# One head's mean of squares: from one fp32 product to two F32R products, placed two slices later

## The chip, the cores and the metric

One NeuronCore of one Trainium2 chip runs the whole program. The metric is the device time of one execution in microseconds (us); lower is better. Engines are named as the profile names them: PE (TensorE's matrix products), PEld (its weight loads), DVE (VectorE), ACT (ScalarE), POOL (GpSimd), SP (SyncE, which only issues DMAs here).

## The reference

The program is a whole network on one sequence of 512 tokens and 1024 features: a first block (convolutions, an RG-LRU, an MLP) and a second one (a gated linear recurrence, an MLP, latent attention, an MLP). The change lies in the recurrence of the second block, `hgrn2_mixer`. Cut to what matters:

```python
q = silu(xn @ w_q);  forget = lb + (1 - lb) * sigmoid(xn @ w_f);  k = 1 - forget;  v = xn @ w_i
# per head (8 heads of 128): o = decayed q.k scores within a chunk @ v, plus q @ carried state
o = o.reshape(1, 512, 8, 128)
o = o * rsqrt(mean(o * o, axis=-1) + 1e-6) * g_norm      # the mean of a head's squared outputs
o = (o * silu(xn @ w_g)).reshape(1, 512, 1024)
return o @ w_o
```

The kernel computes it to fp32's accuracy: a large product is taken as three F32R products of high and low parts (high times high, high times low, low times high).

## The kernel before

Everything is kept with features on the 128 partitions and the 512 tokens along the row. The program of each engine is written out by hand, in order, with semaphores; nothing is scheduled by a compiler. Each engine runs its own list strictly in order, so an instruction that waits holds up all that stands behind it.

Weights come in chunks of 128x2048 through two slots (`raw`, slot 0 and slot 1). ACT makes the high part `w_hi` of a chunk (`split_hi`, L698) when PE is done with the chunk that was in the slot, and POOL makes the low part `w_lo` (`split_lo`, L648) when ACT is done. PE waits for POOL's part (`chunk_in`). In the recurrence a head needs two chunks: slot 0 holds the weights of q and of the forget gate, slot 1 those of the out gate and of v.

The recurrence works on two heads at once. While PE does head h, it fits the projections of head h+1 in as slices; a slice is one of the 8 contraction steps of two output tiles, 6 products of 128x512. `head_pe(h)`:

1. `gates_pe(h+1)`, 8 slices from slot 0, with `mean_out(h-1)` in between: a product with a matrix of ones adds the squares over the partitions (one fp32 product, before the third slice)
2. `turn_values`, `turn_keys` (transposes), `diagonal`
3. seven times `level(h, l)` and behind each a slice of `rest_pe(h+1)` from slot 1; the first of these slices (L2061 behind level 0) is the first reader of slot 1's new chunk
4. `outputs(h)` into bank 6

`level(h, l)` from l=2 on waits until DVE has copied the results of two levels before (`h_g_free`, L1726 and L1729). Head 7 is the last: its slices belong to the output projection (`out_slices`), and only six of them stand ahead of `turn_values`.

DVE, for head h, in `head_dve(h)`: the two gates of head h+1 (L1715, L1716), the copies of the levels (L1726, L1729), then the decays, keys and values of h+1, then `decayed_dve(h+1)`: 14 products (L1794, L1795) and L1799; then the norm of head h: L1834 (needs the inverse root), L1838 (times the out gate), L1840 (low part `OL`, needs ACT's `OH`), L1842 (a scaling of `X` that belongs to the residual). L1838, L1840 and L1842 read two operands from SBUF, as L1794, L1795 and L1799 do; L1777, L1778, L1715, L1716 and L1834 read one of theirs from PSUM.

ACT, for head h: square of head h's outputs (L1032), then for the next head: logarithm and exponential of the mean (`root_out`, L1037, L1039), `split_hi` of slot 1 (L698), `OH` (L1044), `split_hi` of slot 0 (L698), copies of values and keys (L1055, L1057), then gates and decays.

POOL does nothing but the two `split_lo` of each head. The two heads of the loop body and the peeled heads 0 and 7 run the same functions.

Of the kernel before, what the change touches and what calls it, by code (L numbers as in the profile page):

```python
# [7 lines left out]
P = 128  # L8
T = 512
TB = T // P  # L10
D = 1024
KD = D // P
# [17 lines left out]
F32 = mybir.dt.float32  # L30
# [80 lines left out]
def build_program(nc, a, out):  # L111
    ctx = ExitStack()
    with ctx:
# [10 lines left out]
        def sem(name):  # L124
# [69 lines left out]
            ("HE", [P, 7, T], F32), ("HP", [P, T], F32), ("HQD", [P, 2, T], F32), ("HKD", [P, 2, T], F32),  # L194
            ("HEB", [P, 2, T], F32), ("reset", [P, T], F32),
            ("HKT", [P, 3, P], F32), ("HS", [P, 3, P], F32), ("masks", [P, 9 * 256], U8),
            ("FR", [P, T], F32),
        ]
        at_h, made = base + 16 * TILE, []
        for name, shape, dt in tiles_of:  # L200
            made.append(place(name, shape, dt, at_h)[0])
            size = int(np.prod(shape[1:])) * (1 if dt == U8 else 4)
            at_h += size + (-size) % 32
        HR, HZ, HQ, HK, HF, HGATE, HVF, HV, HE, HP, HQD, HKD, HEB, reset, HKT, HS, masks, FR = made

        AH, _ = place("AH", [P, HEADS_M, T], F32R, a_xh)
        AL, _ = place("AL", [P, HEADS_M, T], F32R, S)
# [49 lines left out]
        def s_(name):  # L257

            if name not in S_:
                S_[name] = sem(name)  # L260
            return S_[name]
# [13 lines left out]
            "t_made": ("z_scaled", 8), "t_hi": ("vg_lo", 12), "t_lo": ("v_done", 12), "part_done": ("lru_m", 12),  # L275
            "part_kept": ("lru_done", 15), "u_y": ("mu_add", 7), "u_f": ("xc_done", 8), "u_fh": ("uh_done", 8),
            "u_fl": ("yb_evac", 8), "root_2": ("ch_done", 2), "d_scaled": ("v_part", 36),
        }

        def ff(name, value=0):  # L280
# [3 lines left out]
        def ff_sem(name):  # L284

            return ff(name)[0]
# [406 lines left out]
        def _(act):  # L693
# [335 lines left out]
            def square_out(h):  # L1029

                act.wait_ge(s_("h_o"), h + 1)
                act.activation(tmp[:, 0], ps[:, 6], ACT.Square).then_inc(s_("h_sq"), 1)  # L1032

            def root_out(h):

# [30 lines left out]
                square_out(h)  # L1066

            act.sem_inc(s_("h_ms"), 1)
            gates_act(0, first=True)
            decays_act(0, 0, first=True)  # L1070
            head_act(0, 0, first=True)
# [168 lines left out]
        def _(dve):  # L1240
# [533 lines left out]
            def rest_dve(h, n):  # L1774

                dve.wait_ge(halves, half_at(2 * h + c + 1, 1))
                dve.tensor_tensor(HVF[:], ps[:, 3], HR[:], ALU.mult).then_inc(s_("h_vf"), 1)  # L1777
                dve.tensor_tensor(HGATE[:, n], ps[:, 2], HR[:], ALU.mult).then_inc(s_("h_g0"), 1)  # L1778
# [6 lines left out]
            def decayed_dve(h, n, levels=range(len(LEVELS)), last=True):  # L1785
# [12 lines left out]
                dve.wait_ge(s_("h_eb"), h + 1)  # L1798
                dve.tensor_tensor(HQD[:, n], HQ[:], HEB[:, n], ALU.mult).then_inc(s_("h_qd"), 1)  # L1799

            def keep_dve(s):

                dve.wait_ge(lo_done, FIRST["hwo"] + s + 3)
                for half, w in enumerate((w_hi, w_lo)):
                    dve.tensor_copy(XH[:, 6 + s, half * 256:half * 256 + 256], w[:, s, 7 * 256:8 * 256])\
                        .then_inc(s_("h_kept"), 1)

            def head_dve(h, n, more=True, first=False):
                if more and not first:
                    gates_dve(h + 1)  # L1810
                levels_dve(h, range(2 if first else 0, 4))
                if more:
                    floor_dve(h + 1)
                else:
                    keep_dve(0)
                levels_dve(h, (4,))
                states_dve(h, n)
                levels_dve(h, (5,))
                if more:
                    scan_dve(h + 1)  # L1820
                else:
                    keep_dve(1)
                levels_dve(h, (6,))
                if more:
                    to_end_dve(h + 1, 1 - n)
                    decays_dve(h + 1, range(3))
                levels_dve(h, (7,))
                if more:
                    decays_dve(h + 1, range(3, len(LEVELS)))
                    keys_to_end_dve(h + 1, 1 - n)  # L1830
                    rest_dve(h + 1, 1 - n)
                    decayed_dve(h + 1, 1 - n)
                dve.wait_ge(s_("h_inv"), h + 1)
                dve.scalar_tensor_tensor(tmp[:, 1], ps[:, 6], col("hgrn_g_norm_2"), rst[:, 1], ALU.mult, ALU.mult)\  # L1834
                    .then_inc(s_("h_t1"), 1)
                dve.wait_ge(s_("h_t1"), h + 2)
                dve.wait_ge(s_("hg_done"), h + 1)
                dve.tensor_tensor(tmp[:, 1], tmp[:, 1], HGATE[:, n], ALU.mult).then_inc(s_("h_t2"), 1)  # L1838
                dve.wait_ge(s_("oh_done"), h + 1)
                dve.tensor_tensor(OL[:, bass.ds(h, 1)], tmp[:, 1:2], OH[:, bass.ds(h, 1)].bitcast(F32), ALU.subtract)\  # L1840
                    .then_inc(s_("ho_done"), 1)
                dve.scalar_tensor_tensor(X[:, bass.ds(h, 1)], X[:, bass.ds(h, 1)], dcol("g_final", h),  # L1842
                                         FR[:].rearrange("p (a t) -> p a t", a=1), ALU.mult, ALU.mult)
# [176 lines left out]
        def _(pe):  # L2020
# [298 lines left out]
            def gates_pe(h, ks=range(KD)):  # L2319

                chunk_in(2 * h + c)
                pair(0, 0, XH, XL, lambda k: at("n_hg", "lo", k + 1), ks)
# [88 lines left out]

            def mean_out(h):

                pe.wait_ge(s_("h_sq"), h + 1)
                pe.matmul(ps[:, 7], ones[:], tmp[:, 0], start=True, stop=True).then_inc(s_("h_mean"), 1)

            def head_pe(h, n, more=True, first=False):
                pe.wait_ge(s_("h_q0"), h + 1)
                pe.wait_ge(s_("h_f0"), h + 1)
                if more:  # L2420
                    gates_pe(h + 1, range(2))
                else:
                    out_slices(0, 0, range(2))
                if not first:
                    mean_out(h - 1)
                if more:
                    gates_pe(h + 1, range(2, KD))
                else:
                    out_slices(0, 0, range(2, 6))
                turn_values(h)  # L2430
                turn_keys(h, n)
                diagonal(h)
                pe.wait_ge(s_("h_g0"), h + 1)
                for l in range(len(LEVELS)):
                    level(h, l)
                    if more:
                        rest_pe(h + 1, range(l, l + 1))
                    elif l < 3:
                        out_slices(1, 2, range(l, l + 1))
                    elif l == 3:  # L2440
                        out_slices(0, 0, range(6, 7))
                    else:
                        out_slices(1, 2, range(l - 1, l))
                    if l == 2:
                        states(h, n)
                if more:
                    rest_pe(h + 1, range(7, KD))
                outputs(h, n)
                if not more:
                    out_slices(1, 2, range(6, 7))  # L2450
                    out_slices(2, 4, range(1))
                    mean_out(h)
                    out_slices(2, 4, range(1, 7))
                    for n_ in range(2):
                        out_closed(n_, 2 * n_)
                    out_slices(2, 4, range(7, KD))
# [336 lines left out]
```

## Time and profile before

| | |
|---|---|
| median of 3 runs | 2184.43 us (2183.82 to 2184.82) |
| profiled execution, its own time | 2183.96 us |
| its span, first to last instruction | 2182.2 us |
| around the span | 1.8 us |
| granted TensorE clock, mean | 1.000 (2.4 GHz) |
| PE busy | 2165.0 us, 99% |
| DVE / ACT / POOL busy | 1461.6 / 998.0 / 939.0 us |
| the recurrence, roughly | 874 to 1160 us of the span |

Read it so: PE is busy nearly all the time, so a change shows in the time as far as it takes work or waiting off PE or puts it there. What the other engines do costs nothing until PE has to wait for it.

### The profile page before, as it was taken

What the parts mean: (1) busy time and instruction counts of PE and PEld (TensorE: products, weight loads), DVE (VectorE), ACT (ScalarE), POOL (GpSimd) and SP (SyncE); (2) the same over time, 40 slices, a digit from 0 to 9 for tenths busy, and PEclk for the clock granted to TensorE, in tenths of its full rate; (3) what the DMA queues carried; (4) which work ended last, traced back from release to release, by engine and by line L of the source; (5) the groups of instructions that cost most, each with busy time, mean ns of one, the idle gap of its engine ahead of it and who ended that gap; (6) DMA issues with size and microseconds to landing.
All of it is one profiled execution on the core that took longest, in us unless ns stands there. A gap on an engine that the chain in (4) does not pass through costs nothing.

```text
span 2182.2 us, 30303 instructions
## 1 busy us (share of the span) xinstructions
PE 2165.0 (99%) x11542; PEld 1840.1 (84%) x11542; DVE 1461.6 (67%) x1980; ACT 998.0 (46%) x1364; POOL 939.0 (43%) x263
## 2 busy tenths in 40 slices
PE   8999999999999999999999999999999999999998
PEld 6888888888898897888888898898788888898897
DVE  6999998777556468878877556467666514556463
ACT  5353554525343344666645343344566524343343
POOL 3444455544553554323134553554411244553552
PEclk9999999999999999999999999999999999999999
DMA  5233332422233333222113223332322233323331
GB/s 200 97 106 106 106 116 82 147 90 96 97 102 102 107 97 107 59 78 58 58 58 97 97 97 97 98 110 85 102 53 58 70 85 97 97 97 97 98 112 72
DMA packets 230851, 206.67 MB, mean 95 GB/s; under 512 B 13904, under 2 KB 220368, under 8 KB 230480
## 3 DMA queue, kind: packets, MB, share of 16 engines
q1 hardware_dynamic: 227328, 199.36, 29.5%
q10 hardware_dynamic: 3408, 5.70, 0.7%
q8 instruction: 81, 1.33, 0.3%
q14 instruction: 34, 0.28, 0.0%
HBM read 194.02 MB, written 4.19 MB: 91 GB/s over the span
## 4 chain that ended last, share of the span: by engine, by line
PE 92%; issue 4%; POOL 2%; ACT 1%; DVE 1%; DMA 0%; POOLq 0%; SPq 0%; ACTq 0%; DVEq 0%
PE ps L2028 15%; PE ps L2029 15%; PE ps L2030 15%; PE ps L2261 6%; PE ps L2259 6%; PE ps L2260 6%; PE ps L2061 5%; PE ps L2063 5%; PE ps L2062 5%; PE ps L2388 2%; POOL w_lo L648 2%; PE ps L2595 2%; PE ps L2556 2%; PE ps L2584 1%; PE ps L2691 1%
## 5 line engine op out<-in xcount | busy, mean ns | idle before, releaser
L648 POOL TENSOR_TENSOR w_lo<-raw,w_hi 128x2048 fp32r<-128x2048 f32 x145 | 692.1, 4773 | 944.4 <-ACT w_hi L698 934.5
L698 ACT ACTIVATE w_hi<-raw 128x2048 fp32r<-128x2048 f32 x144 | 275.8, 1915 | 530.4 <-PE ps L2030 354.9
L2028 PE MATMUL ps<-FH,w_hi 128*128 128x512 f32 x528 | 208.3, 395 | 0.0
L2029 PE MATMUL ps<-FL,w_hi 128*128 128x512 f32 x528 | 208.3, 395 | 0.0
L2030 PE MATMUL ps<-FH,w_lo 128*128 128x512 f32 x528 | 208.2, 394 | 0.0
L2028 PE MATMUL ps<-XH,w_hi 128*128 128x512 f32 x512 | 203.2, 397 | 0.0
L2029 PE MATMUL ps<-XL,w_hi 128*128 128x512 f32 x512 | 202.1, 395 | 0.0
L2030 PE MATMUL ps<-XH,w_lo 128*128 128x512 f32 x512 | 202.0, 395 | 0.0
L661 POOL TENSOR_TENSOR w_lo<-raw,w_hi 128x1024 fp32r<-128x1024 f32 x39 | 107.8, 2765 | 198.0 <-ACT w_hi L892 198.0
L1605 DVE TENSOR_TENSOR ps<-ps,rst 128x1024 f32<-128x1024 f32 (+1 forms) x52 | 55.4, 1066 | 171.4 <-PE ps L2030 122.4
L1341 DVE SCALAR_TENSOR_TENSOR ps<-UP,vec,ps 128x512 f32<-128x512 f32 x224 | 148.6, 744 | 0.0
L2061 PE MATMUL ps<-XH,w_hi 128*128 128x512 f32 x352 | 146.2, 415 | 0.9 <-POOL w_lo L648 0.9
L2063 PE MATMUL ps<-XH,w_lo 128*128 128x512 f32 x352 | 138.8, 394 | 0.0
L2062 PE MATMUL ps<-XL,w_hi 128*128 128x512 f32 x352 | 138.7, 394 | 0.0
L891 ACT ACTIVATE w_hi<-raw 128x1024 fp32r<-128x1024 f32 x39 | 41.4, 1061 | 203.8 <-PE ps L2030 166.7
L1582 DVE TENSOR_TENSOR tmp<-ps,SN 128x512 f32<-128x512 f32 x39 | 27.0, 691 | 157.3 <-PE ps L2261 157.3
L671 POOL TENSOR_TENSOR FL<-tmp,FH 128x1024 fp32r<-128x1024 f32 x36 | 90.0, 2501 | 75.8 <-ACT FH L924 75.8
L2028 PEld LDWEIGHTS ps<-FH,w_hi 128*128 128x128 f32 x528 | 99.5, 188 | 23.3
L2030 PEld LDWEIGHTS ps<-FH,w_lo 128*128 128x128 f32 x528 | 99.5, 188 | 23.3
L2029 PEld LDWEIGHTS ps<-FL,w_hi 128*128 128x128 f32 x528 | 99.5, 188 | 23.2
L2029 PEld LDWEIGHTS ps<-XL,w_hi 128*128 128x128 f32 x512 | 96.4, 188 | 23.2 <-issue 0.7
L2028 PEld LDWEIGHTS ps<-XH,w_hi 128*128 128x128 f32 x512 | 96.4, 188 | 23.1 <-issue 0.7
(435 smaller groups left out, 5896.2 us busy)
## 6 DMA issues: line engine op xcount, KB each, us to landing
raw<-in_w SPq DMA_DIRECT2D x64, 512.0 KB, 4.1
raw<-in_mlp_w_up SPq DMA_DIRECT2D x64, 512.0 KB, 4.7
raw<-in_mlp_w_down SPq DMA_DIRECT2D x64, 512.0 KB, 4.3
raw<-in_w_in SPq DMA_DIRECT2D x56, 512.0 KB, 4.6
raw<-in_mla_w_o SPq DMA_DIRECT2D x16, 512.0 KB, 5.1
raw<-in_w_b_out SPq DMA_DIRECT2D x16, 384.0 KB, 3.9
raw<-in_w_a_out SPq DMA_DIRECT2D x8, 512.0 KB, 4.3
raw<-in_w_o SPq DMA_DIRECT2D x8, 512.0 KB, 4.0
```

Source lines behind the costliest of these rows:

```text
L648: pool.tensor_tensor(w_lo[:, s], raw[:, s], w_hi[:, s].bitcast(F32), ALU.subtract)\
L698: act.activation(w_hi[:, s], raw[:, s], ACT.Copy).then_inc(hi_done, 1)
L1341: dve.scalar_tensor_tensor(dst, src, w, acc, ALU.mult, ALU.add).then_inc(cs, 1)
L2028: pe.matmul(dst, his[k], xh[k], start=start and k == 0, stop=False)
L2029: pe.matmul(dst, his[k], xl[k], start=False, stop=False)
L2030: mm = pe.matmul(dst, los[k], xh[k], start=False, stop=stop and k == n - 1)
L2061: pe.matmul(dst, h[n][k], xh[:, k], start=k == 0, stop=False)
L2062: pe.matmul(dst, h[n][k], xl[:, k], start=False, stop=False)
L2063: mm = pe.matmul(dst, l[n][k], xh[:, k], start=False, stop=k == KD - 1)
L2259: pe.matmul(dst, his[k], ah[k], start=start and k == 0, stop=False, skip_group_check=True)
L2260: pe.matmul(dst, his[k], al[k], start=False, stop=False, skip_group_check=True)
L2261: mm = pe.matmul(dst, los[k], ah[k], start=False, stop=k == 3, skip_group_check=True)
```

## The change

The mean of a head's squares is no longer one fp32 product but two F32R ones, of the squares' high part and low part, both with ones in F32R. ACT makes the high part (a copy, right behind the square), DVE the low part (a subtraction, put ahead of `decayed_dve(h+1)`). PE's wait is now for DVE's low part, and `mean_out(h-1)` stands four slices into the gates of the next head and not two. At the end, for head 7, its place stays.

```diff
+            ("FR", [P, T], F32), ("ONES", [P, P], F32R),
+        SQ, _ = place("SQ", [P, 2, T], F32R, a_tmp + 2 * TILE)
...
                 act.activation(tmp[:, 0], ps[:, 6], ACT.Square).then_inc(s_("h_sq"), 1)
+                act.wait_ge(s_("h_sq"), h + 1)
+                act.activation(SQ[:, 0], tmp[:, 0], ACT.Copy).then_inc(ff_sem("h_sqh"), 1)
...
+            act.activation(ONES[:], ones[:], ACT.Copy).then_inc(ff_sem("ones_hi"), 1)
             gates_act(0, first=True)
...
+            def low_square_dve(h):
+
+                dve.wait_ge(*ff("h_sqh", h + 1))
+                dve.tensor_tensor(SQ[:, 1], tmp[:, 0], SQ[:, 0].bitcast(F32), ALU.subtract).then_inc(ff_sem("h_sql"), 1)
...
                     rest_dve(h + 1, 1 - n)
+                low_square_dve(h)
+                if more:
                     decayed_dve(h + 1, 1 - n)
...
             def mean_out(h):
-                pe.wait_ge(s_("h_sq"), h + 1)
-                pe.matmul(ps[:, 7], ones[:], tmp[:, 0], start=True, stop=True).then_inc(s_("h_mean"), 1)
+                pe.wait_ge(*ff("ones_hi", 1))
+                pe.wait_ge(*ff("h_sql", h + 1))
+                pe.matmul(ps[:, 7], ONES[:], SQ[:, 0], start=True, stop=False)
+                pe.matmul(ps[:, 7], ONES[:], SQ[:, 1], start=False, stop=True).then_inc(s_("h_mean"), 1)
...
                 if more:
-                    gates_pe(h + 1, range(2))
+                    gates_pe(h + 1, range(4))
                 else:
-                    out_slices(0, 0, range(2))
+                    out_slices(0, 0, range(4))
                 if not first:
                     mean_out(h - 1)
                 if more:
-                    gates_pe(h + 1, range(2, KD))
+                    gates_pe(h + 1, range(4, KD))
                 else:
-                    out_slices(0, 0, range(2, 6))
+                    out_slices(0, 0, range(4, 6))
```

On PE the place is the gates in the loop body. `XH`, `XL` are the high and low parts of the input, `w_hi`, `w_lo` those of the weights. Before, two slices (12 products) stand between `outputs` and the mean:

```order
L2407 MATMUL ps<-HP,HV 128x128
L2409 MATMUL ps<-HQD,HS 128x128
...
L2061 MATMUL ps<-XH,w_hi 128x512
L2062 MATMUL ps<-XL,w_hi 128x512
L2063 MATMUL ps<-XH,w_lo 128x512
L2414 REGISTER_ALU
L2415 MATMUL ps<-tmp,ones 128x512
L2061 MATMUL ps<-XH,w_hi 128x512
L2062 MATMUL ps<-XL,w_hi 128x512
```

Now four slices (24 products) stand ahead of it:

```order
L2073 MATMUL ps<-XH,w_hi 128x512
L2074 MATMUL ps<-XL,w_hi 128x512
L2075 MATMUL ps<-XH,w_lo 128x512
L2428 MATMUL ps<-SQ,ONES 128x512
L2429 MATMUL ps<-SQ,ONES 128x512
L2073 MATMUL ps<-XH,w_hi 128x512
L2074 MATMUL ps<-XL,w_hi 128x512
```

So 12 products moved from behind the mean to ahead of it, and all that waits for the mean moved with it.

On ACT the place is the end of a head and the beginning of the next, with the line numbers of the changed kernel (before: L1032, L1037, L1039, L698, L1044):

```order
L1034 ACTIVATE tmp<-ps 128x512
L1036 ACTIVATE SQ<-tmp 128x512
L1041 ACTIVATE rst<-ps,vec 128x512
L1043 ACTIVATE rst<-rst 128x512
L698 ISA
L699 ISA
L700 ACTIVATE w_hi<-raw 128x2048
L1048 ISA
L1048 ACTIVATE OH<-tmp 128x512
```

The copy is new; `split_hi` of slot 1 still stands behind the exponential of the mean's root.

On DVE the place is ahead of the 14 products of `decayed_dve` (before: L1778, then L1794):

```order
L1782 TENSOR_TENSOR HVF<-ps,HR 128x512
L1783 TENSOR_TENSOR HGATE<-ps,HR 128x512
L1809 TENSOR_TENSOR SQ<-tmp,SQ 128x512
L1798 ISA
L1799 TENSOR_TENSOR HE<-HE,HK 128x4x64
L1800 TENSOR_TENSOR HE<-HE,HQ 128x4x64
```

L1809 is new and moves everything behind it back.

## Rows read from the trace of the kernel before

**Rows 1.** The page, busy time of each engine.

```profile
PE 2165.0 (99%) x11542; PEld 1840.1 (84%) x11542; DVE 1461.6 (67%) x1980; ACT 998.0 (46%) x1364; POOL 939.0 (43%) x263
```

**Rows 2.** Waits of PE, 880 to 1170: waiter, releaser, total us, times, longest.

```profile
PE ps L2061 <- POOL w_lo L648: 0.9, 1, 0.9
```

**Rows 3.** Timeline of PE, one head: start, us, engine, line, op.

```profile
1086.20 0.39 PE L2063 MATMUL ps<-XH,w_lo 128*128 128x512 f32 x1
1086.42 1.02 PE L2415 MATMUL ps<-tmp,ones 128*128 128x512 f32 x2
...
1087.51 0.39 PE L2062 MATMUL ps<-XL,w_hi 128*128 128x512 f32 x1
...
1095.42 0.39 PE L2063 MATMUL ps<-XH,w_lo 128*128 128x512 f32 x1
...
1098.12 0.47 PE L2061 MATMUL ps<-XH,w_hi 128*128 128x512 f32 x1
...
1101.87 1.00 PE L2388 MATMUL ps<-HE 128*128 128x64 f32 x8
```

**Rows 4.** Timeline of ACT, the same head.

```profile
1084.38 0.58 ACT L1032 ACTIVATE tmp<-ps 128x512 f32<-128x512 f32 x1
1087.48 0.69 ACT L1037 ACTIVATE rst<-ps,vec 128x512 f32<-128x512 f32 x1 [2.53 <-PE ps L2415]
...
1088.74 1.91 ACT L698 ACTIVATE w_hi<-raw 128x2048 fp32r<-128x2048 f32 x1
1096.06 0.63 ACT L1044 ACTIVATE OH<-tmp 128x512 f32 x1 [5.41 <-DVE tmp L1838]
1096.60 1.89 ACT L698 ACTIVATE w_hi<-raw 128x2048 fp32r<-128x2048 f32 x1
```

**Rows 5.** Timeline of POOL, the same head.

```profile
1090.73 4.65 POOL L648 TENSOR_TENSOR w_lo<-raw,w_hi 128x2048 fp32r<-128x2048 f32 x1 [20.83 <-ACT w_hi L698]
1098.57 4.60 POOL L648 TENSOR_TENSOR w_lo<-raw,w_hi 128x2048 fp32r<-128x2048 f32 x1 [3.19 <-ACT w_hi L698]
```

**Rows 6.** Timeline of DVE, the same head.

```profile
1084.93 0.68 DVE L1778 TENSOR_TENSOR HGATE<-ps,HR 128x512 f32<-128x512 f32 x1
1085.52 0.41 DVE L1794 TENSOR_TENSOR HE<-HE,HK 128x256 f32<-128x256 f32 x1
...
1091.60 4.33 DVE L1838 TENSOR_TENSOR tmp<-tmp,HGATE 128x512 f32<-128x512 f32 x1
1096.85 0.69 DVE L1840 TENSOR_TENSOR OL<-tmp,OH 128x512 f32 x1 [0.92 <-ACT OH L1044]
1097.46 0.74 DVE L1842 SCALAR_TENSOR_TENSOR X<-X,vec,FR 128x512 f32 x1
...
1100.17 1.05 DVE L1729 COPY_PREDICATED HP<-masks,ps 128x256 f32<-128x256 uint8 x2
```

**Rows 7.** Timeline of POOL and of DVE from 889: one POOL instruction that took longer.

```profile
889.24 8.51 POOL L648 TENSOR_TENSOR w_lo<-raw,w_hi 128x2048 fp32r<-128x2048 f32 x1 [7.28 <-ACT w_hi L698]
889.29 0.42 DVE L1771 TENSOR_TENSOR HE<-HF 128x256 f32<-128x256 f32 x1
...
893.25 0.68 DVE L1777 TENSOR_TENSOR HVF<-ps,HR 128x512 f32<-128x512 f32 x1
```

**Rows 8.** Timeline of POOL and of DVE at 421, in an earlier stage.

```profile
421.43 4.86 POOL L648 TENSOR_TENSOR w_lo<-raw,w_hi 128x2048 fp32r<-128x2048 f32 x1 [3.78 <-ACT w_hi L698]
421.13 5.70 DVE L1480 TENSOR_TENSOR XL<-CO,XH 128x512 fp32r<-128x512 f32 x2
```

**Rows 9.** Timeline of POOL and PE, last head: slot 1's chunk and its first slice.

```profile
1123.99 4.62 POOL L648 TENSOR_TENSOR w_lo<-raw,w_hi 128x2048 fp32r<-128x2048 f32 x1 [20.83 <-ACT w_hi L698]
1128.66 0.51 PE L2028 MATMUL ps<-OH,w_hi 128*128 128x512 f32 x1
```

**Rows 10.** Timeline of POOL and of DVE, end of head 0.

```profile
924.11 5.34 POOL L648 TENSOR_TENSOR w_lo<-raw,w_hi 128x2048 fp32r<-128x2048 f32 x1 [15.65 <-ACT w_hi L698]
925.67 4.33 DVE L1838 TENSOR_TENSOR tmp<-tmp,HGATE 128x512 f32<-128x512 f32 x1
```

More of the change, by code:

```diff
@@ L196, in build_program @@
             ("HKT", [P, 3, P], F32), ("HS", [P, 3, P], F32), ("masks", [P, 9 * 256], U8),
-            ("FR", [P, T], F32),
+            ("FR", [P, T], F32), ("ONES", [P, P], F32R),
         ]
+        SQ, _ = place("SQ", [P, 2, T], F32R, a_tmp + 2 * TILE)
         at_h, made = base + 16 * TILE, []
@@ L203, in build_program @@
             at_h += size + (-size) % 32
-        HR, HZ, HQ, HK, HF, HGATE, HVF, HV, HE, HP, HQD, HKD, HEB, reset, HKT, HS, masks, FR = made
+        HR, HZ, HQ, HK, HF, HGATE, HVF, HV, HE, HP, HQD, HKD, HEB, reset, HKT, HS, masks, FR, ONES = made
         AH, _ = place("AH", [P, HEADS_M, T], F32R, a_xh)
@@ L277, in build_program @@
             "u_fl": ("yb_evac", 8), "root_2": ("ch_done", 2), "d_scaled": ("v_part", 36),
+            "h_sqh": ("mu_mm", 1), "h_sql": ("mu_done", 1), "ones_hi": ("var_mm", 1),
         }
```

## The prediction

> **What bounds the kernel now.** I read the page first: PE is busy 2165.0 of 2182.2 us, 99% of the span [rows 1]. So a gain can only be PE's own work, and a loss is any wait that reaches PE. The waits of the recurrence come next: PE waits there for anything nameable only once, 0.9 us for POOL's low part [rows 2]. Then I read the timelines of the four engines over one head, because the change is small on PE and larger in what it moves on the others. The head from 1086 on stands for the rest: the same POOL instruction comes 33.26 us later in the next head [rows 5, 9]. Two things are to be seen.
>
> First, PE's list. The product of the mean starts at 1086.42, and the second product behind it at 1087.51; the next 34 products take 7.91 us, 0.233 each [rows 3].
>
> Second, DVE and POOL get in each other's way. L1838 takes 4.33 us where L1840, of the same form, takes 0.69 [rows 6]. It began at 1091.60, POOL's subtraction ran from 1090.73 to 1095.38 [rows 5], and L1838 ended at 1095.93, 0.55 behind it. So a DVE instruction with two operands in SBUF stands still while POOL's subtraction runs. L1834, with an operand in PSUM, does not. Today this costs nothing: PE has other work.
>
> **The change part by part.** *The product itself.* The fp32 mean costs 1087.51 - 1086.42 - 0.23 = 0.86 us. Two F32R products cost 0.46. That is 0.40 less, 8 times in the program: 3.2 us saved on PE, the whole of the intended gain. The copy of the ones (128x128) at the start of the recurrence lies in ACT's time before the first gates are scaled; without that cover it would cost less than L1044's 0.63 [rows 4], once.
>
> *The mean's date.* 12 products move ahead of it, 2.78 us. It starts at 1089.20 and its second product ends at 1089.20 + 0.23 + 0.39 = 1089.82 (before: 1087.44). L1037 starts 0.04 behind, at 1089.86, where it was 1087.48 [rows 4]: 2.38 later. `split_hi` of slot 1 is queued behind it on ACT and moves with it, and POOL's first subtraction with that: from 1090.73 to 1093.11 and, at 4.6 us, to 1097.7.
>
> *The squares' parts.* ACT ends the square at 1084.96 [rows 4]; the copy, priced as L1044 at 0.63, ends at 1085.62. DVE starts 0.16 behind (as L1840 behind L1044: 1096.69 to 1096.85), at 1085.78, and gives way after 0.60. The products of `decayed_dve` begin at 1086.38 and not at 1085.52 [rows 6]: all of DVE's list moves by 0.86. PE has its low part at 1086.5, long before 1089.20, so the new wait itself costs nothing; the cover is the two added slices. At the end, for head 7, there are only two slices, and the low part would be there some 0.4 us before PE.
>
> *Who is late next.* L1838 now starts at 1091.60 + 0.86 = 1092.46, before POOL (1093.11), and is done at 1093.15: 2.8 us earlier than before. `OH` follows on ACT, 1093.3 to 1093.9. L1840 could go at 1094.07 but now it is the one that POOL holds, to 1097.7, and it ends 0.55 later, at 1098.25, where it ended at 1097.54. Behind it on DVE stand L1842, the gates of the next head, and the level copies.
>
> Meanwhile ACT is free for `split_hi` of slot 0 as soon as PE has left the slot. The last product of the gates starts at 1095.42 - 0.40 and ends at 1095.41; ACT works to 1097.4, POOL's second subtraction is due at 1097.45. Before, ACT came to it only at 1096.60, and POOL began at 1098.57 [rows 5], 3.19 us after its first one ended and clear of L1840 and L1842. Now it is due 0.25 us before the first one ends. POOL's two instructions, 9.2 us together, touch, and DVE has two two-operand instructions to get in at the joint.
>
> If POOL goes on with the second at the joint or takes the gap of some hundredths of a us between L1840 and L1842, then L1842 stands from 1098.2 to the end of the second subtraction, 1102.75, and ends 0.55 later, at 1103.3; before it ended at 1098.20 [rows 6]. All of DVE behind it is 5.1 us late: the first L1729 ends at 1100.17 + 0.43 + 5.1 = 1105.7. PE stands at level 2, which it began at 1101.87 [rows 3], until 1105.8. That is 3.9 to 4.1 us more than before for such a head, PE's 0.40 already in it; I take 4.0.
>
> Does POOL get in? The rows are of two kinds. At 889.24 a POOL instruction was due while DVE ran two-operand instructions back to back; it took 8.51 us, that is, it began work at 893.2, when DVE came to L1777 with its operand in PSUM [rows 7]: the 11 DVE instructions from 889.29 on all went ahead of it. At 421.43 it took 4.86, so it began 0.26 us after it was due, between two L1480 that stood back to back; the second ended behind it, both took 5.70 [rows 8]. So either may win. In rows 7 nearly all of DVE's instructions have 256 elements, in rows 8 they have 512, as L1840 and L1842 do. I take POOL as the winner.
>
> The Trainium skill has a rule for this ("SBUF — State Buffer", section Who interferes with whom): whoever issues first gets the shared port for the whole instruction, and the other blocks until it finishes. Rows 8 go with it, rows 7 against it. By the rule L1840 (waiting since 1094.07) would come ahead of POOL's second, and the second (due 1097.45) ahead of L1842: the same case and the same sum.
>
> *How often.* Both `split_hi` stand in heads 1 to 6, so six pairs. The first is different: there POOL would be due at 924.11 + 2.38 = 926.49 and L1838 at 925.67 + 0.86 = 926.53 [rows 10]. If POOL is first there, L1838 is held as before, `OH` is late, slot 0's split and the values' copy behind it on ACT come 1.7 us later than before, and PE loses about that; if not, it is a pair like the others. I take 1.7. Five pairs at 4.0 are 20.0.
>
> *The last head.* PE's first slice from slot 1 began at 1128.66, 0.05 behind POOL's end at 1128.61 [rows 9]: here POOL was already just in time, because only six slices stand ahead. POOL comes 2.38 later, so does the slice; a wait of 0.2 behind it falls away. 2.1 us lost, the saving of that head's mean included. In the other heads the slice stands at 1098.12 - 0.40 = 1097.72 against POOL's 1097.7 + 0.05: up to 0.1 each, hidden where PE stands at level 2 anyway. The mean of head 7 saves 0.40.
>
> Sum: 20.0 + 1.7 + 2.1 - 0.4 = +23.4 us on the profiled execution's 2183.96 us (span 2182.2 and 1.8 around it), which lies 0.5 us below the median of the runs, 2184.43. I predict 2207.
>
> **The rivals.** *No collision that counts (not slower).* DVE gets in at the joint with L1840 and L1842 both, as in rows 7. L1840 ends at 1098.25, L1842 starts at 1098.17 and not at 1097.46, the first L1729 ends at 1101.3, PE wants level 2 at 1101.5: a tie, up to 0.1 us. Then a head costs -0.40 + 0.1 + 0.1 = -0.2, five of them -1.0; the first pair +1.7 or nearly nothing, the last head 2.1, the last mean -0.4: +0.7 to +2.4, 2185 to 2187. It decides at one point: who holds the port between 1097.7 and 1098.2 of a head. Rows 7 speak for it, rows 8 against.
>
> *The saving alone.* If all the waits that I add (the last head too) were hidden, 3.2 us would be gained: 2181.2. Against it: rows 9, where nothing hides POOL.
>
> *POOL ahead of L1838 in all heads.* It needs 0.65 us less between them than I find. Then L1838 is held to 1098.25, every head is like the first pair, 1.7 each: +12, 2196.
>
> **How the numbers follow.** A measurement here tells a change from none from about 0.2%, 4.4 us. Collision: 0.52, its own range 2200 to 2213. DVE wins at both: 0.36, 2183 to 2188. Saving alone: 0.05. POOL ahead of L1838, or a collision in some heads only: 0.07, 2190 to 2199. The range has to hold both main cases: 2183 to 2213. Slower takes the first, the last and a rest of the second: 0.6. Same 0.37; faster 0.03, since 3.2 us is less than 4.4.
>
> **What would show it.** PE's waits in the recurrence: some 4 us at level 2 of heads 2 to 6, for DVE's copy; in the last head 2.4 us for POOL at the first slice from slot 1. L1842's counterpart at 5 us or L1840's at 8; L1838's back at 0.69. POOL's two instructions touching, 9.2 us. The two new products 0.23 apart. If instead both DVE instructions stand between POOL's two, the collision step is wrong and the rest holds. The whole is wrong if L1840's counterpart is never held, that is, if ACT or POOL comes at other dates than the chain from the mean gives.

## The result and the profile after

The changed kernel takes **2226.59 us** (median of 4 runs, 2225.38 to 2227.31), the kernel before, in the same session, 2184.12 us (4 runs, 2183.72 to 2184.82). The ratio is 1.0194 with a 95% interval of 1.0178 to 1.0210: 1.9% slower. The forecast was 2207 in a range of 2183 to 2213. The direction was right, the size was not: the loss is 42 us and not 23. The profiled execution took 2225.38 us with a span of 2223.6, 41.4 us more than the span before.

The page of the changed kernel, busy time of each engine (it answers to [rows 1]):

```profile
PE 2179.0 (98%) x11542; PEld 1853.6 (83%) x11542; DVE 1492.0 (67%) x1988; ACT 1004.2 (45%) x1373; POOL 940.2 (42%) x263
```

PE has as many instructions as before, and they should be 3.2 us shorter. Yet PE is busy 14 us longer. So there are two losses: PE stands (that is, it waits with nothing to do), and PE works more slowly.

Waits of PE in the recurrence, 870 to 1210, in the changed kernel: waiter, releaser, total us, times, longest (answers to [rows 2]):

```profile
PE ps L2400 <- DVE HP L1734: 24.5, 6, 4.1
PE ps L2040 <- POOL w_lo L650: 2.5, 1, 2.5
PE ps L2073 <- POOL w_lo L650: 1.3, 2, 1.0
```

Six stands at level 2, one for each pair of POOL instructions, and one in the last head. The next four fences show what leads to such a stand. First POOL, ACT and DVE of the changed kernel, the head from 1082 on (they answer to [rows 5], [rows 4] and [rows 6]; L1850, L1852 and L1854 are L1838, L1840 and L1842 of before):

```profile
1085.29 9.57 POOL L650 TENSOR_TENSOR w_lo<-raw,w_hi 128x2048 fp32r<-128x2048 f32 x2 [30.45 <-ACT w_hi L700]
```

```profile
1082.05 0.69 ACT L1041 ACTIVATE rst<-ps,vec 128x512 f32<-128x512 f32 x1 [4.24 <-PE ps L2429]
...
1083.31 1.90 ACT L700 ACTIVATE w_hi<-raw 128x2048 fp32r<-128x2048 f32 x1
1085.35 0.63 ACT L1048 ACTIVATE OH<-tmp 128x512 f32 x1
1087.65 1.91 ACT L700 ACTIVATE w_hi<-raw 128x2048 fp32r<-128x2048 f32 x1 [1.67 <-PE ps L2075]
```

```profile
1083.75 0.74 DVE L1846 SCALAR_TENSOR_TENSOR tmp<-ps,vec,rst 128x512 f32<-128x512 f32 x1
1084.53 0.69 DVE L1850 TENSOR_TENSOR tmp<-tmp,HGATE 128x512 f32<-128x512 f32 x1
1086.14 4.29 DVE L1852 TENSOR_TENSOR OL<-tmp,OH 128x512 f32 x1 [0.92 <-ACT OH L1048]
1090.35 5.06 DVE L1854 SCALAR_TENSOR_TENSOR X<-X,vec,FR 128x512 f32 x1
1095.33 0.68 DVE L1720 TENSOR_TENSOR HZ<-ps,HR 128x512 f32<-128x512 f32 x1
```

POOL's instruction begins 3.24 us behind the mean's root, as before. Its two instructions are one block of 9.57 us now. L1850 runs free in 0.69. L1852 comes 0.85 us behind POOL's start and is held for the first of the two, L1854 for the second. The gates of the next head (L1720, operand in PSUM) start only at 1095.33.

The timeline of PE in the changed kernel, the stand at level 2 and what follows (answers to the last row of [rows 3]):

```profile
1093.24 0.39 PE L2074 MATMUL ps<-XL,w_hi 128*128 128x512 f32 x1
1093.47 0.39 PE L2075 MATMUL ps<-XH,w_lo 128*128 128x512 f32 x1
1097.94 1.96 PE L2400 MATMUL ps<-HE 128*128 128x64 f32 x8 [4.08 <-DVE HP L1734]
...
1100.24 0.63 PE L2074 MATMUL ps<-XL,w_hi 128*128 128x512 f32 x1
1100.66 0.63 PE L2075 MATMUL ps<-XH,w_lo 128*128 128x512 f32 x1
1101.09 0.63 PE L2073 MATMUL ps<-XH,w_hi 128*128 128x512 f32 x1
```

Behind the stand the same products start 0.43 us apart (1100.24, 1100.66, 1101.09), ahead of it 0.23. Busy time by stretch in the changed kernel: after the stretch and its sum the columns are PE, PEld, DVE, ACT and POOL, then the granted TensorE clock, the share of DMA and GB/s:

```profile
930.00:937.50 7.50, 4.71 (x28) 3.72 (x26) 7.50 (x4) 2.39 (x4) 6.00 (x2) 1.00 0.52 143
937.50:944.40 6.90, 5.32 (x19) 4.74 (x20) 2.52 (x6) 6.27 (x8) 0.00 (x0) 0.51 0.55 151
...
978.50:985.30 6.80, 6.50 (x25) 5.93 (x25) 1.37 (x4) 5.69 (x7) 0.00 (x0) 0.50 0.40 108
...
1019.50:1022.90 3.40, 3.40 (x13) 2.92 (x13) 0.81 (x3) 3.33 (x5) 0.00 (x0) 0.50 0.56 146
...
1057.00:1063.80 6.80, 5.87 (x22) 5.30 (x22) 1.86 (x5) 6.14 (x8) 0.00 (x0) 0.50 0.48 132
...
1098.00:1104.80 6.80, 6.80 (x26) 6.22 (x27) 1.14 (x3) 5.33 (x7) 0.00 (x0) 0.50 0.22 74
...
1138.90:1142.30 3.40, 3.40 (x12) 2.86 (x11) 0.76 (x2) 3.35 (x5) 0.00 (x0) 0.50 0.28 97
...
1169.60:1173.00 3.40, 3.40 (x14) 2.93 (x13) 1.77 (x4) 0.00 (x0) 0.00 (x0) 0.51 0.80 247
```

The granted clock is 1.00 in the stretches between them and half of it, that is 1.2 GHz and not 2.4, in seven stretches, each at the end of a stand or behind it. The numbers behind the comma are PE's busy time in them: 5.32 + 6.50 + 3.40 + 5.87 + 6.80 + 3.40 + 3.40 = 34.7 us of work at half rate. How much of it is loss? The products of 512 columns start 0.43 us apart and not 0.23, so a little less than half is lost, 0.20 of 0.43. At 0.46 that is 16.0 us; experiment 4 measures the six falls in the heads directly and finds the same share.

So the account of the profiled execution is: six stands at level 2, +24.5; the last head's wait, +2.5; the other waits for POOL, 1.3 where 0.9 was, +0.4; half rate, +16.0; eight means at 0.40 less, -3.2; and 0.35 for each of the six stands beyond the wait that the profile shows, +2.1. The last term is the rest of a head's length in experiment 4, where the clock did not fall. Nearly half of it is a matter of counting: the wait is counted from the end of the product ahead of it, but the start of L2400 lies 4.47 us behind the start of that product (1093.47 to 1097.94) where 0.23 is usual, which makes 4.24 and not 4.08. The sum is +42.3. The spans differ by 41.4, but this execution reached the recurrence 0.7 us earlier than the one before (POOL's first start behind 870 us is at 876.63, before at 877.34), so from there to the end it lost 42.1.

### The profile page after: what moved, and what is told of

It reads as the page before. It is cut to its first block, busy times and chain, and to the rows that moved or that the text cites. A ratio compares the mean times of both kernels' runs of the same rounds, so it can differ in the third digit from the quotient of the medians.

```text
span 2223.6 us, 30325 instructions
## 1 busy us (share of the span) xinstructions
PE 2179.0 (98%) x11542; PEld 1853.6 (83%) x11542; DVE 1492.0 (67%) x1988; ACT 1004.2 (45%) x1373; POOL 940.2 (42%) x263
## 4 chain that ended last, share of the span: by engine, by line
PE 79%; issue 15%; POOL 3%; DVE 1%; ACT 1%; DMA 0%; POOLq 0%; ACTq 0%; SPq 0%; DVEq 0%
PE ps L2040 14%; PE ps L2042 14%; PE ps L2041 14%; PE ps L2273 6%; PE ps L2271 6%; PE ps L2272 6%; POOL w_lo L650 3%; PE ps L2075 3%; PE ps L2074 3%; PE ps L2073 3%; PE ps L2609 2%; PE ps L2570 1%; PE ps L2598 1%; PE ps L2705 1%; PE ps L2707 1%
## 5 line engine op out<-in xcount | busy, mean ns | idle before, releaser
L893 ACT ACTIVATE w_hi<-raw 128x1024 fp32r<-128x1024 f32 x39 | 41.4, 1061 | 203.7 <-PE ps L2042 166.7
```

## The experiments

Two things are to be shown: that the stands come from the date of POOL's instructions, and that nearly all of the rest of the loss is the clock. All ratios below are to the kernel before, run on the same chip, with their 95% interval.

**1. Only the mean back to two slices.**

```diff
-                    gates_pe(h + 1, range(4))
+                    gates_pe(h + 1, range(2))
...
-                    gates_pe(h + 1, range(4, KD))
+                    gates_pe(h + 1, range(2, KD))
```

(and the same for `out_slices` in the last head.)

> The changed kernel with the mean put back behind two slices (12 products) of the next gates, and behind two in the last head; the split of the squares and the two F32R products stay. Theory (the mean's date moves POOL's first low part into the second, and all the loss comes from that): the mean starts about 1086.5 and ends about 1087.1, POOL begins its first low part about 1090.4 and ends about 1095.1, its second stands clear at about 1098.3; the X scaling takes 0.74 again, PE has no 4 us stand and the granted clock stays at 1.00. Time 2181 to 2183. Rival (the split's DVE instruction, 0.86 us ahead of the decayed products, is enough by itself): stands of about 4 us at level 2 stay, 2215 to 2227.

Measured: 2187.38 us, ratio 1.0014 (1.0005 to 1.0023). The big loss is gone, and with it every fall of the clock in the recurrence. But the time is not 1 to 3 us below the kernel before, it is 3 us above: the theory's number (2181 to 2183) missed. POOL, one instruction of DVE and PE's waits in this kernel:

```profile
1059.21 5.67 POOL L650 TENSOR_TENSOR w_lo<-raw,w_hi 128x2048 fp32r<-128x2048 f32 x1 [20.20 <-ACT w_hi L700]
...
1092.85 5.65 POOL L650 TENSOR_TENSOR w_lo<-raw,w_hi 128x2048 fp32r<-128x2048 f32 x1 [20.18 <-ACT w_hi L700]
1101.69 4.57 POOL L650 TENSOR_TENSOR w_lo<-raw,w_hi 128x2048 fp32r<-128x2048 f32 x1 [3.20 <-ACT w_hi L700]
```

```profile
1093.94 0.75 DVE L1846 SCALAR_TENSOR_TENSOR tmp<-ps,vec,rst 128x512 f32<-128x512 f32 x1
```

```profile
PE ps L2400 <- ACT HV L1059: 2.0, 6, 0.4
```

A head takes 1092.85 - 1059.21 = 33.64 us where it took 33.26. POOL's first instruction takes 5.65 us, some 1.1 longer than its usual 4.6: it was due while DVE's two-operand products ran back to back, which do so 0.86 us later than before. It ended at 1098.50, so at 4.6 us it got to work about 1093.9, when DVE came to L1846, with its operand in PSUM. On ACT, `OH`, the split of slot 0 and `HV` are late behind it, and PE waits at level 1 for `HV`. The squares' low part came 0.14 us too late for the mean as well (its two products start 0.29 and 0.31 behind the ones ahead of them, where 0.23 is usual). So the split of the squares has a price of its own, which more than uses up its gain.

**2. Only the mean's date, in the kernel before** (fp32 mean behind four slices, no split).

```diff
-                    gates_pe(h + 1, range(2))
+                    gates_pe(h + 1, range(4))
...
-                    gates_pe(h + 1, range(2, KD))
+                    gates_pe(h + 1, range(4, KD))
```

> The kernel before with its fp32 mean moved to behind four slices (24 products); no split, nothing added on ACT or DVE. Theory of two parts (date and DVE's delay of 0.86 us are both needed): DVE is not late, so the product with the gate is done by 1092.3, the low part of the output due at 1093.1, 0.4 us ahead of POOL, which the fp32 mean sends off at about 1093.5. So DVE gets both of its instructions through, POOL takes its turn at 1093.5 to 1094.5 and ends at 1098.1 to 1099.1; PE waits up to 1 us a head for it at slot 1's first slice and 2.8 us in the last head: 2188 to 2195, granted clock 1.00. Rival (the date alone is the cause): the low part of the output is held by POOL as in the changed kernel, PE stands 4 us a head, the clock falls behind it: 2225 to 2232.

Measured: 2230.38 us, ratio 1.0213 (1.0199 to 1.0226). My theory of two parts fell, the rival stands: the date alone brings on the whole loss. DVE and POOL of this kernel:

```profile
1086.97 0.75 DVE L1834 SCALAR_TENSOR_TENSOR tmp<-ps,vec,rst 128x512 f32<-128x512 f32 x1 [0.74 <-ACT rst L1039]
...
1089.42 4.54 DVE L1840 TENSOR_TENSOR OL<-tmp,OH 128x512 f32 x1 [0.97 <-ACT OH L1044]
1093.88 5.05 DVE L1842 SCALAR_TENSOR_TENSOR X<-X,vec,FR 128x512 f32 x1
```

```profile
1088.82 9.57 POOL L648 TENSOR_TENSOR w_lo<-raw,w_hi 128x2048 fp32r<-128x2048 f32 x2 [31.29 <-ACT w_hi L698]
```

What I had missed is the first row: DVE, though not late by 0.86, now waits 0.74 us for the mean's root itself. Both chains then start from the root, POOL's and that to `OL`, and POOL's is the shorter one by 0.6 us. The kernel is 3.8 us slower than the changed one, of which 8 x 0.40 = 3.2 is the dearer product (the two were measured in different sessions).

**3. The date with ACT's order changed: the split of slot 1 ahead of the root.**

```diff
+                if not first:
+                    split_hi(2 * h + c + 3, 1)
                 if not first:
                     root_out(h - 1)
-                if not first:
-                    split_hi(2 * h + c + 3, 1)
                     out_act(h - 1)
```

> The changed kernel with ACT's split of slot 1 put ahead of the root of the mean, so that POOL's first low part no longer waits for the mean. The mean stays behind four slices. Theory: POOL is due at about 1087.5, in the middle of the decayed products; either it gets in when DVE comes to its PSUM operand at 1091.8 and ends at about 1096.4, then the product with the gate is held to 1096.9, the second low part comes at about 1099.6, clear of the first, and a head is 0.2 us shorter than before: 2181 to 2184; or it gets in at 1087.5 and holds one decayed product for 4.6 us, DVE is 1 to 2 us late at the level copies: 2185 to 2192. Both without a 4 us stand and with the clock at 1.00. Rival (POOL's place relative to the mean is not what matters): the 4 us stands stay, 2215 to 2227.

Measured: 2196.35 us, ratio 1.0056 (1.0042 to 1.0070). No pairs touch any more, as the theory had it, but it was slower than both of its ways. DVE of this kernel, and PE's waits:

```profile
1093.05 0.42 DVE L1799 TENSOR_TENSOR HE<-HE,HQ 128x256 f32<-128x256 f32 x1
1093.39 4.85 DVE L1798 TENSOR_TENSOR HE<-HE,HK 128x256 f32<-128x256 f32 x1
```

```profile
PE ps L2386 <- DVE tmp L1845: 7.0, 6, 3.4
```

POOL, due at 1093.29, got in between two products that stood back to back, and the next was held. PE then waits at the diagonal for L1845 (`h_t1`), the longest time, 3.4 us, in the last head, and behind that stand alone the clock fell (0.50 from 1136.6 to 1143.4). In one head of the seven it went the other way: POOL, due at 990.95, took 8.48 us and all of DVE's products went ahead. The instructions are the same, and POOL is due at the same place within about 0.1 us (1.36 us behind the start of the first product there, 1.24 in the head shown), yet both outcomes occur.

**4. PE kept busy in the stand.** 16 products into part of a bank that nothing reads, ahead of the wait.

```diff
+                if l == 2 and busy:
+                    pe.wait_ge(s_("h_kt_c"), h + 1)
+                    for _ in range(busy):
+                        pe.matmul(ps[:, 7, 384:512], ident[:], ident[:], start=True, stop=True)
                 if l >= 2:
                     pe.wait_ge(s_("h_g_free"), 8 * h + l)
```

> The changed kernel with 16 extra fp32 products (ident by ident, 128x128) on PE ahead of its wait at level 2 in heads 1 to 6, into columns 384 to 511 of bank 7, which nothing reads; about 3.6 us of the 4.08 us stand, so PE is busy where it stood. Theory (of the 41.4 us, some 24.1 are net waits and some 17.3 are products at half rate after the fall of the granted clock, which the idle stand brings on): the clock stays at 1.00 behind these six stands, the 15.6 us lost there come back, one fall behind the last head's wait stays: 2209 to 2212. Rival (the clock falls for another reason, or the time is not lost to the clock): 2224 to 2230.

Measured: 2211.57 us, ratio 1.0129 (1.0113 to 1.0144), inside what the theory gave. PE of this kernel at level 2:

```profile
1084.75 3.73 PE L2398 MATMUL ps<-ident 128*128 128x128 f32 x32
1088.99 1.10 PE L2404 MATMUL ps<-HE 128*128 128x64 f32 x8 [0.51 <-DVE HP L1734]
```

DVE is as late as before and level 2 begins as late, but PE stands 0.5 us and not 4.08, and the granted clock stays at 1.00 in the whole of the recurrence. PE does more work and the kernel is 15.0 us faster than the changed one. Take the six heads with a stand, from POOL's first start in the first of them to its start in the last head. They take 1150.89 - 926.68 = 224.21 us here and 1164.56 - 925.97 = 238.59 in the changed kernel. The difference, 14.4 us, is the price of the six falls, 0.46 of the 31.3 us of work at half rate there (the expectation took half, 15.6). In this execution the fall behind the last head's wait was missing too, and that stretch is 1.6 us shorter. So the loss beyond the stands is the clock's, by experiment: 16.0 us in the profiled executions, 15.0 between the medians.

A head takes 37.30 us here (POOL's starts at 1039.03 and 1076.33), 4.03 more than before and 0.35 more than 33.27 - 0.40 + 4.08. That is the 0.35 of the account above: 0.16 is the counting of the wait, 0.10 is that level 2 begins more slowly behind a stand (0.91 us from L2404 to the next product where 0.81 is usual), the rest is open.

**5. PE kept busy for half of the stand**: the same with 8 products.

> As the busy stand, with 8 extra products instead of 16: PE works 1.8 us more and then stands about 2.3 us, in each of heads 1 to 6. The kernel with 16 took 2211.6, the changed kernel 2226.6. Theory (a shorter stand brings the clock down in fewer places or for a shorter time): between them, 2213 to 2223. Rival A (2.3 us are too short for a fall): 2210 to 2213. Rival B (any stand brings the full fall): 2224 to 2228.

Measured: 2220.89 us, ratio 1.0163 (1.0150 to 1.0177), between the two. Busy time by stretch, some head's length to a row:

```profile
930.00:970.00 40.00, 37.42 (x199) 32.44 (x199) 30.88 (x54) 20.30 (x27) 9.18 (x3) 0.91 0.20 53
970.00:1010.00 40.00, 37.71 (x218) 32.90 (x217) 32.43 (x54) 22.31 (x28) 10.74 (x3) 0.96 0.19 53
1010.00:1050.00 40.00, 37.70 (x226) 32.89 (x224) 33.99 (x55) 23.84 (x31) 12.29 (x4) 1.00 0.20 54
1050.00:1090.00 40.00, 37.70 (x225) 32.89 (x224) 34.00 (x54) 21.34 (x28) 12.29 (x3) 1.00 0.27 72
```

Each of these rows holds one of the six stands of 2.3 us. In two the clock is below 1.00 for a part of the stretch, in two it isn't. Over all six it fell behind four. The five executions of this kernel took from 2215.92 to 2221.08 us, the fastest with the highest mean clock, 0.996 against 0.994 to 0.995.

**6. The held X scaling taken out of the way**: moved ahead of the low part of the squares.

```diff
+                dve.scalar_tensor_tensor(X[:, bass.ds(h, 1)], X[:, bass.ds(h, 1)], dcol("g_final", h),
+                                         FR[:].rearrange("p (a t) -> p a t", a=1), ALU.mult, ALU.mult)
                 low_square_dve(h)
...
                     .then_inc(s_("ho_done"), 1)
-                dve.scalar_tensor_tensor(X[:, bass.ds(h, 1)], X[:, bass.ds(h, 1)], dcol("g_final", h),
-                                         FR[:].rearrange("p (a t) -> p a t", a=1), ALU.mult, ALU.mult)
```

> The changed kernel with DVE's X scaling (the instruction that POOL's second low part holds for 5.06 us) moved from behind the low part of the output to ahead of the low part of the squares, where POOL is idle. Theory (the stand at level 2 is made by the X scaling being held): the low part of the output is still held to POOL's end, but the gates of the next head, with an operand in PSUM, follow it at once; no 4 us stand, clock 1.00, the last head still waits 2.5 us: 2183 to 2187. In between: the scaling makes the product with the gate due 0.6 us later, 0.15 us ahead of POOL; if POOL is first there, that product is held, everything behind it on ACT and DVE comes some 1.7 us later: 2188 to 2192. Rival (the hold of the low part of the output alone makes the stand): 2205 to 2227.

Measured: 2189.13 us, ratio 1.0029 (1.0018 to 1.0040). That is 37 us less than the changed kernel, 2 us above the theory's range and in the range between (2188 to 2192). DVE and POOL of this kernel:

```profile
1096.38 4.08 DVE L1854 TENSOR_TENSOR OL<-tmp,OH 128x512 f32 x1 [0.90 <-ACT OH L1048]
1100.38 0.68 DVE L1720 TENSOR_TENSOR HZ<-ps,HR 128x512 f32<-128x512 f32 x1
```

```profile
1095.05 9.86 POOL L650 TENSOR_TENSOR w_lo<-raw,w_hi 128x2048 fp32r<-128x2048 f32 x2 [23.33 <-ACT w_hi L700]
```

POOL's two instructions touch as before, and the low part of the output is held as before. Only its successor is now one with an operand in PSUM, and it starts at once, in the middle of POOL's block. So it is the second hold, of the X scaling, that makes the stand. What is left of the loss is the first pair and the last head. In the first pair, and only there, the case in between came about: POOL is ahead, the product with the gate is held (4.68 us), and PE waits 2.0 us for `HV`. The last head waits 2.8 us and has a fall of the clock behind it.

**7. Another order on ACT that parts POOL's two instructions**: the copies `HV` and `HKT` ahead of the split of slot 0; the mean stays behind four slices.

```diff
-                if more and not first:
-                    split_hi(2 * h + c + 4, 0)
                 act.wait_ge(s_("h_vt"), h + 1)
...
+                if more and not first:
+                    split_hi(2 * h + c + 4, 0)
```

> The changed kernel with one order changed on ACT: the copies of the turned values and keys (HV, HKT) ahead of the split of slot 0, not behind it. The mean stays behind four slices. Theory: the copies wait for PE's transposes, so the split of slot 0 ends some 1.8 us later and POOL's second low part begins about 1.7 us behind the end of its first; in that gap both the low part of the output and the X scaling are over. No instruction of 5 us on DVE, no stand at level 2, clock 1.00; what stays is the last head's wait of 2.5 us: 2182 to 2186. Rival (it is enough that the first low part holds DVE): stands of 2 us or more stay, 2197 to 2227.

Measured: 2186.01 us, ratio 1.0008 (0.9999 to 1.0017), at the top of the range that was expected. POOL and DVE of this kernel:

```profile
1092.92 4.59 POOL L650 TENSOR_TENSOR w_lo<-raw,w_hi 128x2048 fp32r<-128x2048 f32 x1 [22.73 <-ACT w_hi L700]
1098.58 4.59 POOL L650 TENSOR_TENSOR w_lo<-raw,w_hi 128x2048 fp32r<-128x2048 f32 x1 [1.07 <-ACT w_hi L700]
```

```profile
1093.77 4.29 DVE L1852 TENSOR_TENSOR OL<-tmp,OH 128x512 f32 x1 [0.92 <-ACT OH L1048]
1097.98 0.74 DVE L1854 SCALAR_TENSOR_TENSOR X<-X,vec,FR 128x512 f32 x1
```

A gap of 1.07 us between POOL's two is enough: the X scaling takes 0.74 in it. The first hold is as long as in the changed kernel, and costs nothing. A head takes 32.99 us (POOL's starts at 1059.93 and 1092.92), 0.27 less than before. Over six heads that is 1.6 us. More than that is lost in the last head, which waits 2.5 us for POOL and has a fall of the clock of some 1.6 us behind it; the time is 1.9 us above the kernel before.

**8. The same order with the mean behind two slices.**

> The kernel with the mean behind two slices (first experiment), and HV, HKT ahead of slot 0's split on ACT. Theory (the first experiment's 3 us over the kernel before are PE's wait of 0.5 us a head at level 1 for the copy HV, which stood behind a late split, and 0.14 us a head for the squares' low part): the wait for HV goes, the one for the low part stays; 33.0 to 33.1 us a head against 33.26 before; 2182 to 2184. Rival (another thing than the place of HV makes the head longer): 2186 to 2188.

Measured: 2183.60 us, ratio 0.9997 (0.9988 to 1.0006). The wait for `HV` is gone, a head takes 33.0 us, as the theory had it, and the time is inside its range.

**9. The same order with three slices.**

> As the one before, with the mean behind three slices: PE no longer comes ahead of the squares' low part, POOL's first low part is due 0.55 us later than with two. Theory: a head is 0.4 us shorter than in the kernel before, 32.86 us, the last head loses about 1 to 1.5 us to POOL: 2181 to 2183. Rival (three slices already bring on the touch of POOL's two instructions or a late DVE): over 2186.

Measured: 2184.44 us, ratio 1.0001 (0.9992 to 1.0010), above the theory's range. The last head waits 1.2 us, as expected, but the other heads take 33.2 us and not 32.86. PE of this kernel at level 2:

```profile
1034.34 0.40 PE L2075 MATMUL ps<-XH,w_lo 128*128 128x512 f32 x1
1034.80 1.10 PE L2400 MATMUL ps<-HE 128*128 128x64 f32 x8
```

Level 2 starts 0.46 us behind the product ahead of it, where 0.23 is usual, and takes 0.10 more to its next product. These 0.33 are the difference. The view of waits does not name them, since they lie almost wholly under the end of the product ahead. DVE's first L1734 runs there from 1034.22, behind an L1850 that POOL held for 4.54 us: the copy is just late for PE.

**10. Three slices with ACT's order as it was.**

> The changed kernel with the mean behind three slices, ACT's order as it was. Theory (what decides is whether POOL's first low part comes before or after the product with the gate): with three slices POOL is first by less than 0.1 us, that product is held to POOL's end, the low part of the output and the X scaling run behind it in the clear, POOL's two instructions do not touch; OH, the split of slot 0 and HV are late, PE waits some 0.7 us a head at level 1: 2186 to 2190, clock 1.00. Rival (the loss grows with the date, half of it at half the way): 2200 to 2210.

Measured: 2188.31 us, ratio 1.0020 (1.0011 to 1.0029). DVE and PE's waits of this kernel:

```profile
1095.26 4.55 DVE L1850 TENSOR_TENSOR tmp<-tmp,HGATE 128x512 f32<-128x512 f32 x1
1100.73 0.69 DVE L1852 TENSOR_TENSOR OL<-tmp,OH 128x512 f32 x1 [0.92 <-ACT OH L1048]
1101.34 0.75 DVE L1854 SCALAR_TENSOR_TENSOR X<-X,vec,FR 128x512 f32 x1
```

```profile
PE ps L2400 <- ACT HV L1059: 4.6, 6, 1.1
```

The time is inside the theory's range. With two slices 3 us are lost, with three 4, with four 42. The step is between three and four, where L1850 gets ahead of POOL and the pair closes up.

**11. The version to which the runs point.** As experiment 8, and the last mean one slice of six products later.

> The version to which the runs point: both F32R products behind two slices, HV and HKT ahead of slot 0's split on ACT, and for head 7 the mean one slice of six products later, since PE waited 0.6 us there for the squares' low part. Theory: that wait goes, all else as with two slices and HV first (2183.6): 2182.5 to 2183.5, at or just beyond what a measurement can tell from the kernel before. Rival (PE's end of the stage waits for head 7's output instead): 2184 or more.

Measured: 2183.20 us, ratio 0.9996 (0.9987 to 1.0005). It beats the changed kernel by 43 us and can't be told from the kernel before. The reason that I gave for the last edit was wrong: PE's wait of 0.6 us for the squares' low part is still there, since it belongs to the first mean and not to the last.

## Why the prediction was right or wrong

**The product** was right: 0.40 us less for each mean. In the changed kernel the two products and the next one start 0.23 apart (1081.39, 1081.62, 1081.85). A part of the saving is also seen in experiments 7 and 8, where a head is 0.27 and 0.25 us shorter than before.

**The chain from the mean** was right. POOL starts 3.24 us behind the root (3.25 before), L1850 takes 0.69, L1852 is held 4.29, L1854 5.06, POOL's two touch, 9.57 us together (the forecast says 9.2, but its own dates, 1093.11 to 1102.75, make 9.6). POOL did win at the joint, in all six heads. The reason for which I took POOL, that DVE's instructions have 512 elements there and not 256, does not hold: in experiment 3 they have 256, and POOL got in in six heads and had to wait in one. That the choice came out right was in part luck.

**The stand at level 2** was right: "some 4 us" was 4.08, and a pair at 4.0, the mean's 0.40 already in it, is what a head without a fall of the clock costs, 37.30 - 33.27 = 4.03 (experiment 4). The last head's wait was right, 2.5 us for 2.4.

**The first pair** was put at 1.7, by a tie of 0.04 us; DVE was first and it was a pair like the others, 4.0, so 2.3 more. Without the clock the account is +26.3, and the forecast was +23.4.

**The step that failed is the last term, the granted clock.** In the prediction it reads: "no row prices that; the bound is 1 us a head, from 0.23 us more for each of some four products". I had chosen zero for it. Measured, half rate lasts 3.4 to 6.9 us at or behind a stand, in which the table counts 12 to 26 of PE's instructions, and costs 1.5 to 3.2 us each time, 16.0 in all. Experiment 4 shows that the stand brings it on: with the same dates and PE at work in the stand, 15.0 us come back. The word "bound" was not earned. What had to be bounded was the time at half rate, and the recurrence of before has no stretch from which to take it; the four products were made up. The Trainium skill ("TensorE: Matmul & The Clock Gate", section Terms) prices a fall as the time at less than full rate by the share of pulses left out. With the table's 37.5 us at half rate that is an estimate of 18.8. The rows give 16.0: PE still stood for 2.8 us of that time, and a product takes 0.43 us and not twice 0.23. So the rule is 2.8 us too high here, but its form, time and not a number of products, is what my bound lacked.

**Of the rivals,** "no collision that counts", with a chance of 0.36, did not come about in any of the six heads. Its time, 2185 to 2187, is close to that of experiments 1 and 7 (2187.4 and 2186.0), where the pair is parted by other means. "More than I price" named both of the things that happened, at 2.3 and at 6 us; they were worth 2.3 and 16.0.

**What the prediction took for a cause and was none:** the 0.86 us of the squares' low part on DVE. With four slices it does next to nothing, for DVE would wait 0.74 us for the root anyway (experiment 2). With two slices, where I had not priced it, a head is 0.4 us longer although its mean is 0.40 shorter (experiment 1). So the change has no part that gains by itself in this order of ACT's: the product saves 3.2 us, and the split that it needs takes about twice that.

## What to carry to other kernels

Where PE is the bound, price a stand of some us at more than its length: look whether the granted clock falls behind it, and count a little less than half of the whole time that PE then works at half rate. A transfer of dates is best followed on every engine from the one instruction that moved, here the root, and the order in which two chains from it arrive at a shared resource decides more than their lengths. And a resource taken twice in a row does harm that twice the same use with a gap of 1 us does not: look for what brings the two uses together.

## What the runs showed of the hardware

**Stands and the clock.** All six stands of 4.08 us had half rate behind them, in the changed kernel as in experiment 2. Of the stands of 2.3 to 3.4 us there were 13: the last head's in the changed kernel (2.5) and in experiments 2 to 7 (2.6, 3.4, 2.5, 2.5, 2.8, 2.5), and six of 2.3 in experiment 5. Ten were followed by half rate, three were not: two of the six, and the 2.5 us of experiment 4. Behind the recurrence's shorter waits, of up to 1.3 us and one of 2.0 (experiment 6), it never fell. The time at half rate was some 3.4 or 6.8 us, and did not go by the length of the stand. All this is counted in one profiled execution of each kernel; the median of experiment 4's four executions is some 1.5 us above the profiled one, which had no fall.

**POOL and DVE.** A held DVE instruction of 512 elements with two operands in SBUF ended 0.55 us behind POOL's (experiments 7 and 10). Who goes first when POOL becomes due while such DVE instructions stand back to back isn't settled by the place in the program: in experiment 3 POOL got in at once in six heads and waited for all of them in one (8.48 us); in experiment 1 it waited some 1.1 us each time. The Trainium skill ("SBUF — State Buffer", section Who interferes with whom) says that the order of issue decides who blocks: the first has the port, the other waits for its end. The held instructions agree with it; the waits of POOL of 1.1 and 3.9 us behind a row of DVE instructions, all but the first of which began later than POOL was due, do not.
